# In the page queue the value pages stand six key groups behind instead of five

## What is computed

```python
def past_kv(i):
    kp = cache_k[i, page_table].reshape(db, past_len, MOBA_HEADS, HEAD_DIM)
    vp = cache_v[i, page_table].reshape(db, past_len, MOBA_HEADS, HEAD_DIM)
    return kp, vp
...
k_mean = jnp.mean(kb.astype(jnp.float32), axis=3)          # blocks of 256 positions
gate = jnp.einsum('bhtd,bhnd->bhtn', qh.astype(jnp.float32), k_mean)
_, sel = lax.top_k(gate, n_sel)                            # 3 past blocks and the own one
...
logits = (jnp.einsum('bhqd,bhqrsd->bhqrs', qi, kg) * scale - slopes[:, None, None, None] * dist)
p = jax.nn.softmax(logits.reshape(bsz, h, qc, r * MOBA_BLOCK), axis=-1).reshape(logits.shape)
return jnp.einsum('bhqrs,bhqrsd->bhqd', p, vg.astype(jnp.float32)).astype(q.dtype)
```

## Time and profile before

| what | value |
|---|---|
| median of 3 runs | 1305.23 us (1303.71 to 1305.43) |
| the profiled execution, device time | 1302.96 us |
| its span, first to last instruction | 1301.2 us |
| PE (TensorE matmul) busy | 1143.8 us, 88% |
| DVE (VectorE) busy | 722.9 us, 56% |
| ACT (ScalarE) busy | 563.0 us, 43% |
| POOL (GpSimd) busy | 294.1 us, 23% |
| mean granted TensorE clock | 0.937 of 2.4 GHz |

### The profile page before, as it was taken

One profiled execution on the slowest core, in us unless ns is written; L12 is line 12 of the kernel. 1 busy time (PEld: TensorE's weight loads), 2 busy tenths in 40 slices (PEclk: granted clock), 3 DMA queues, 4 the chain that ended last, 5 costly groups with the idle time before them and its releaser, 6 DMA issues.

```text
span 1301.2 us, 20535 instructions
## 1 busy us (share of the span) xinstructions
PE 1143.8 (88%) x7143; PEld 1005.1 (77%) x7143; DVE 722.9 (56%) x1216; ACT 563.0 (43%) x886; POOL 294.1 (23%) x262
## 2 busy tenths in 40 slices
PE   5999689778788788767989999997999799999995
PEld 4999689455455454443889999996999699999994
DVE  4743624566656766642466666345556566666333
ACT  3447301344454555433364444335334554443434
POOL 8201015101454554453220000022101310000011
PEclk9999959888989999985989999998999899999997
DMA  7334100335657666735425345343444244544421
GB/s 229 114 103 157 35 1 1 119 133 186 210 196 242 226 207 215 246 110 162 135 85 174 129 139 181 116 134 118 129 153 149 95 130 147 175 129 135 151 78 40
DMA packets 119124, 182.62 MB, mean 140 GB/s; under 512 B 6128, under 2 KB 59471, under 8 KB 118990
## 3 DMA queue, kind: packets, MB, share of 16 engines
q1 hardware_dynamic: 116274, 173.30, 40.6%
q0 software_dynamic: 2784, 8.47, 2.4%
HBM read 176.12 MB, written 5.63 MB: 140 GB/s over the span
## 4 chain that ended last, share of the span: by engine, by line
PE 46%; ACT 3%; DVE 2%; POOL 1%; issue 0%; DVEq 0%; POOLq 0%
PE bank L1618 46%; POOL xl L617 1%; ACT xres L953 1%; DVE xres L1068 1%; ACT hi L674 1%; ACT xh L674 1%; PE bank L2015 0%; ACT L944 0%; PE bank L2083 0%; DVE xres L1480 0%; DVE hraw L1068 0%; PE bank L2005 0%; DVE lo L1061 0%; DVE lnt L1068 0%; ACT lnt L946 0%
## 5 line engine op out<-in xcount | busy, mean ns | idle before, releaser
L1618 PE MATMUL bank<-xh,hi 128*128 128x320 f32 x1184 | 373.7, 316 | 40.0 <-POOL xl L617 26.4
L1618 PE MATMUL bank<-xl,hi 128*128 128x320 f32 x1184 | 371.3, 314 | 0.0
L1618 PE MATMUL bank<-xh,lo 128*128 128x320 f32 x1184 | 370.9, 313 | 0.0
L1061 DVE TENSOR_TENSOR lo<-raw,hi 128x2048 fp32r<-128x2048 f32 x102 | 241.3, 2366 | 188.6 <-ACT hi L674 188.6
L1618 PEld LDWEIGHTS bank<-xh,hi 128*128 128x128 f32 x1184 | 227.5, 192 | 43.1 <-issue 31.2
L674 ACT ACTIVATE hi<-raw 128x2048 fp32r (+1 forms) x102 | 194.8, 1909 | 107.6 <-PE bank L1618 107.6
L1618 PEld LDWEIGHTS bank<-xl,hi 128*128 128x128 f32 x1184 | 227.5, 192 | 0.1
L1618 PEld LDWEIGHTS bank<-xh,lo 128*128 128x128 f32 x1184 | 227.2, 192 | 0.0
L594 POOL TENSOR_TENSOR lo<-vring,hi 128x1024 fp32r<-128x1024 f32 x60 | 145.0, 2418 | 176.1 <-ACT hi L674 176.0
L1068 DVE TENSOR_TENSOR kTl<-bank,kTh 128x512 fp32r<-128x512 f32 x128 | 88.1, 689 | 103.6 <-ACT kTh L674 101.6
L1618 PE MATMUL bank<-hh,hi 128*128 128x320 f32 x416 | 129.3, 311 | 1.3 <-DVE hraw L1068 1.3
(11 more groups left out here) (376 smaller groups left out, 1500.1 us busy)
## 6 DMA issues: line engine op xcount, KB each, us to landing
raw<-w_up SPq DMA_DIRECT2D x44, 1024.0 KB
kring<-cache_k SPq DMA_DIRECT2D x128, 256.0 KB, 3.7
vring<-cache_v SPq DMA_DIRECT2D x128, 256.0 KB, 3.4
raw<-w_down SPq DMA_DIRECT2D x8, 2048.0 KB
raw<-w_in_mix SPq DMA_DIRECT2D x7, 2048.0 KB
raw<-w_in_sc SPq DMA_DIRECT2D x8, 1024.0 KB
raw<-w_down SPq DMA_DIRECT2D x4, 1536.0 KB
raw<-w_out_mix SPq DMA_DIRECT2D x2, 2048.0 KB
```

Source lines behind the costliest of these rows:

```text
L1061: dve.tensor_tensor(lo[:, p], weight(n)[:, :, 256 * p:256 * p + 256], hi[:, p], ALU.subtract)\
L1618: return pe.matmul(out, lhsT, rhs, start=start, stop=stop, **kw)
```

## The change

The value loads move back by one iteration of the loop: iteration n issues key group n and then value group n-6. No other engine's program changes.

```diff
-            for n in range(4 * NB + 5):
+            for n in range(4 * NB + 6):
                 if n < 4 * NB:
                     after(sp_, "kT_mm", 4 * n - 4)
                     load_pages(kring, a["cache_k"][0], "k_in", n)
-                if n == 5:
+                if n == 6:
                     PE.wait(sp_, "po1")
-                if n >= 5:
-                    lo_ready(sp_, 2 * (n - 5) - 3)
-                    load_pages(vring, a["cache_v"][0], "v_in", n - 5)
+                if n >= 6:
+                    lo_ready(sp_, 2 * (n - 6) - 3)
+                    load_pages(vring, a["cache_v"][0], "v_in", n - 6)
```

## The result

The changed kernel takes 1291.59 us (1288.85 to 1295.05, 4 runs) where the kernel before takes 1304.47 us (4 runs): ratio 0.9914, 95% interval 0.989 to 0.9938. It is faster, by 12.9 us, inside the range of 1268 to 1293, but the forecast was 28.5 us of gain. Less than half of it came.

The account below looks back on a forecast made before the run. It took TensorE's key-page waits, from key loads held behind value loads in SyncE's in-order queue, as the bound. 24.8 + 10.0 - 6.3 + 0 = 28.5 us off 1305.23 gave 1276.7, range 1268 to 1293.

Parts of the forecast that it names:

- Part 1: SyncE's queue: key groups are issued 4.3 us earlier, so all 24.8 us of TensorE's key-page waits go.
- Part 2: TensorE at u=14: the slow clock behind six long key waits goes, 10.0 us gained, bounds 0 and 10.0.
- Part 3: Value groups go 2.4 us later; TensorE waits 1.05 us a round, -6.3 us over six rounds, bounds -2.4 and -9.6.
- no wait, 0.1 us to spare: Value group 11: its low half is ready by 425.0, `values(22)` comes at 425.15, so TensorE does not wait.
- Part 4: VectorE's burst beside GpSimd's shifted low-half steps: taken as 0, with -6 to +6 us over the rounds.
- Part 5: Start and end: nothing waits for value group 0, and the tail keeps its length.
- A: Value pages take over part of the key wait, TensorE waits 1.6 us a round, low clock stays: 1290, chance 0.20.
- estimate of up to 1.8 us more: Page landings under high HBM load: 1.8 us longer would cut the gain to 17.7, so 1287.5, within A's chance.
- B: Slower: ScalarE's wait reaches TensorE for each of 24 value groups, 58 us lost against 34.8 gained: 1328, chance 0.06.
- C: Nothing gained: VectorE's low keys take the place of TensorE's key wait at once: 1305, chance 0.05.
- D: More gained: the softmax burst also gets free of GpSimd, 39.5 us in all: 1266, chance 0.05.

Follow-up runs that it names:

- experiment 2: Changed kernel with each value group loaded in two halves, one ahead of the key group and one behind it: 1266.32 us, ratio 0.9711.
- experiment 3: Kernel before the change, value groups still five behind, with a third place for value groups in the buffer: 1263.42 us, ratio 0.9691.
- second profile: The changed kernel run and profiled once more, unedited: 1292.97 us, ratio 0.9899.
- experiment 4: Kernel of experiment 3, third place kept, with value groups six behind the key groups instead of five: 1283.69 us, ratio 0.9845.

## Why the prediction was wrong, step by step

**Part 1, key pages: right.** Key loads went 1.33 us behind their transposes, and all key waits are gone. With nothing late in their place (experiments 2 and 3) the clock is 1.00 and five rounds fall from 191.2 to 162.4 us, 5.8 us a round. That is what parts 1 and 2 together had: 34.8 us for six rounds, 5.8 each.

**Part 2, the clock: right for the old waits, wrong for the changed kernel.** The clock no longer falls at u=14, but it falls behind new waits in three of five rounds. The part had that case as its lower bound, and the sum took the full 10.0 us. In five rounds TensorE's busy time fell by 3.5 us (157.8 to 154.3) where the kernel without late pages has 9.8 (to 148.0). So 6.3 us in five rounds, 1.3 a round, did not come.

**Part 3, value pages later: the mechanism right, the size wrong.** The forecast was 1.05 us a round. Against the round of 32.5 us the changed kernel loses 36.5 - 32.5 = 4.0 us, and 3.6 in its second profile. Of the 4.0, 2.8 us are idle time of TensorE and 1.3 the slow clock of part 2. Together that is the whole difference: 3 us a round more than forecast over six rounds are 18 us, and the missing gain is 28.5 - 12.9 = 15.6. Two steps of the working of part 3 failed, and the clock followed from them.

The first is the wait at u=0. The issue time and the landing (6.2 us) were as worked out, but I followed only the first value half into TensorE and allowed 0.1 us for each hand-over of the low keys. ScalarE had in the same 2.8 us the queries, two high-key steps and the second value half in its queue, and the low queries then met GpSimd's two steps in a row. TensorE waited 2.11 us, and the next key steps of VectorE, with which the softmax burst begins, were late as well. That VectorE's low queries took 1.26 us is not what was new: they take 1.27 in experiment 2 too, where TensorE does not wait for them. u=14 to u=2 came to 9.1 us on average instead of the 8.2 forecast (7.12 undisturbed plus 1.05).

The second is "no wait, 0.1 us to spare" for value group 11. I asked when `values(22)` needs its low half and not when ScalarE comes to the step. ScalarE waited 2.24 us, `kT_hi(68)` behind it was late, and the burst waited for it, which no `values` step shows. u=2 to u=6 is 10.8 us undisturbed and was 10.8 to 13.7 in the changed kernel's rounds. Of the 2.24 us, 1.5 come from the slow landing of this one group (7.55 us against 6.07); in the other rounds, the first left out, ScalarE waited 0.8 to 2.3 us at this place, with landings of 5.8 to 6.3 us.

**Part 4, the burst beside GpSimd: 0 was near enough, for a reason not given.** Rank steps rose from 14.7 to 20.6 us in all and copies fell from 13.9 to 9.3. These two nearly cancel, though not in where they fall. The low queries were overlooked: 2.0 us in all before and 7.9 after, since they now run beside GpSimd. VectorE's busy time in the five rounds rose from 123.6 to 128.8 us, but it is 127.9 in experiment 2 with its shorter rounds, so this is not what the changed kernel lost.

**Part 5, start and end: right within a us or two.** From the first transpose of key group 31 to the end of the last value product it is 56.0 us before and 57.1 after. The first round lost more than the others: value group 2 was on hand 8.3 us after its issue, TensorE waited 4.5 us, and the clock fell behind it. In the second profile, with 6.9 us, it waited 3.2 us there.

**Rivals.** A gave 1290 and the time is 1291.6. Its sign, a low clock behind new waits, came in three rounds of five, and its waits were if anything too small (1.6 us a round against 2.8). Its cause did not: landings hardly lengthened, the profile puts one value DMA at 3.6 us in the median after and 3.4 before, and the loss is as large in the second profile. That A's number fits is in part luck, a larger wait against a clock that fell less often. The Trainium skill (DMA: Bandwidth & Descriptors, Latency and other measured facts) puts an access to HBM at 0.2 us on average and 2 us at high load, from which the prediction's estimate of up to 1.8 us more was made. With 261 GB/s in experiment 2, against 219 before, the trace doesn't show it: one value DMA takes 3.5 us there. B, C and D did not happen; B's passing-through of ScalarE's waits did in part, twice a round.

**The range.** Its lower end was said to be all bounds on the good side, but these add up to 24.8 + 10.0 - 2.4 + 6 = 38.4 us, which gives 1266.8 and not 1268. The bounds on the bad side give 24.8 + 0 - 9.6 - 6 = 9.2 us, 1296, above the range's upper end. The measured gain of 12.9 us lies between the two, but the idle time that part 3 speaks of was 2.8 us a round, outside of its bound of 1.6.

## What to carry to other kernels

When loads of two kinds share one in-order queue, work out for each kind when it is wanted by the first engine that takes it, and what stands behind that step on that engine; the consumer at the end of the chain may have slack that the engine in the middle has not. Swapping whole groups only chooses which kind is late. Loading the half that is wanted first ahead of the other kind's group, and the half wanted last behind it, made neither late, with no more room, and took 38 us off where the swap took 13.

A new wait can also cost more than its idle time, by the clock behind it. In the changed kernel's trace four waits at u=3 took 2.4 to 2.6 us, and the clock was low (0.55 to 0.60) behind three of them; in experiment 4 it stayed at 1.00 behind all three waits of 2.4 us. What tells the two apart is not shown, so a forecast has to price both.

## What the runs showed of the hardware

VectorE's small SBUF steps are slow beside GpSimd's tensor_tensor: two rank steps of 32x64 take 0.35 us alone, 2.25 us beside one GpSimd step of 2.4 us, 3.73 us beside two. Taking GpSimd's long steps away was worth 23 us of 1263, about 17 of them in VectorE's burst. The Trainium skill (GPSIMD Engine Reference, Architecture) has a read port that GpSimd shares with VectorE; the runs agree, but they show only the times, not the port. I had not expected that the loss is this large in a kernel whose GpSimd is busy 23% of the span.
